# Three taps of a 31-tap depthwise convolution go from TensorE to VectorE

## The chip, the cores and the metric

The kernel runs on one core of one Trainium2 chip, in one launch, with float32 inputs and outputs. The metric is the device time of one execution in microseconds (us). Of the engines, PE is TensorE, DVE is VectorE, ACT is ScalarE, POOL is GpSimd, and SP issues the transfers.

## The reference

The reference is a first block (modulation, a two-branch mixer, a gated feed-forward part), and then two more layers (gated delta rule, block attention, each with a SwiGLU part). The change lies in one branch of the first mixer, on 256 positions of 512 channels:

```python
h = layer_norm(x) * (1.0 + sc1[:, None]) + sh1[:, None]
proj = h @ w_in[l]
a_val, a_gate, u_pool, gate_a, gate_b = jnp.split(proj, [...], axis=-1)
ya = a_val * jax.nn.sigmoid(a_gate)
ya = causal_dwconv(ya, w_dw_a[l], b_dw_a[l])      # 31 taps, 512 channels, one filter per channel
ya = jax.nn.silu(layer_norm(ya, ln_a_g[l], ln_a_b[l]))
ya = ya @ w_pw_a[l]
...                                               # a pooling branch makes yb
merged = jax.nn.sigmoid(gate_a) * ya + jax.nn.sigmoid(gate_b) * yb
mix = merged @ w_out[l]
```

Everything after `mix` depends on it: the other layers work on this block's output.

## The kernel before

Activations lie with channels on the 128 partitions and the 256 positions along the row, in tiles of 128 x 256. Weights stream in as units of 128 x 1024 float32 in the order of a fixed plan, into a ring of eleven buffers `raw`. For each unit ACT makes a rounded copy `hi` (`high`, line 1119) and DVE the remainder `lo = raw - hi` (`low`, line 1652), each into a ring of five slots. A product is then three matmuls, hi by hi, hi by lo and lo by hi (`three`, line 542). One output tile of 128 x 256 takes 8 x 3 = 24 matmuls. DVE runs `low` four units ahead of the unit that PE is at, and `high` for a unit waits until PE has finished the unit five before it. Some buffers of the ring hold rows of the modulation matrix, which DVE alone consumes (`ada`, line 1639).

No scheduler orders the work: each engine's queue is written out by hand, and the engines meet at semaphores. In the stage around the change the loop over `n` from 0 to 7 makes the input-projection tiles 20 to 27 (they are called so here), whose outputs are the gates of the pooling branch. Beside each tile some taps of the convolution are done.

A tap on PE is four float32 matmuls (line 644), one per channel tile: the stationary operand is a 128 x 128 diagonal matrix with the tap's weights, which ACT makes from the identity (line 1195), the moving operand the shifted input `ypad` (in the profile Z). They all add up in two PSUM banks. The trace records a float32 matmul as two instructions. `TAPS_AT[n]` says how many taps stand behind which tile; its entries 7 to 12 belong to the tiles 22 to 27. A tap on DVE is four operations `cv = ypad * w + cv` on 128 x 256 (line 1767; `cv` is B in the profile), each waiting for the one of the tap before on the same channel tile. Both engines work at the same convolution without waiting for each other; at the stage's end DVE adds the two PSUM banks to `cv` (line 1824), for which it waits for the last tap of both. Then comes a layer norm over channels (PE line 549 for the mean), in which PE is kept running with matmuls whose results nobody reads (`spin`, line 537), then SiLU, and the next product (`pw`).

In the loop DVE's queue for tile 20+n holds: `low`, for n = 7 also an `ada`, then tap or taps, then the multiplication of one pooled output by its gate (line 1818), which waits for ACT's sigmoid (line 1230) of an earlier tile. ACT's holds: `high`, the diagonals of the taps behind this tile, the sigmoid of the tile.

Of the kernel before, what the change touches and what calls it, by code (L numbers as in the profile page):

```python
# [262 lines left out]
class Marks:  # L263
# [12 lines left out]
    def up(self, name, key=0):  # L276
        chain = SEM_OF.get(name, name)
        n = self.count[chain] = self.count.get(chain, 0) + 1
        if self.counting:
            assert (name, key) not in self.place, (name, key)  # L280
            self.place[name, key] = n
        assert self.place[name, key] == n, (name, key)
        return self.sem(name), 1

    def at(self, name, key=0):
        return self.sem(name), 1 if self.counting else self.place[name, key]
# [33 lines left out]
def program(nc, wts, head, vecs, csts, rows, xtok, xT, low_dram, inv_dram, out):  # L320
    with ExitStack() as ctx:
# [37 lines left out]
        def V(name, i=0, n=1):  # L359
            return vec[:, VOFF[name] + i:VOFF[name] + i + n]  # L360
# [7 lines left out]
        up, at = marks.up, marks.at  # L368
# [17 lines left out]
        def acc(b0, n):  # L386
            return bank[(b0 + n // 2) % 8][:, (n % 2) * S:(n % 2) * S + S]
# [7 lines left out]
        def pair(b):  # L395
            return bank[b][:, :].rearrange("p (a b) -> p a b", a=2)
# [64 lines left out]
        xt = B[4][:, :, :].rearrange("p a b -> p (a b)").rearrange("p (c n) -> p c n", c=2)  # L461
        xh = B[5]
        xst, xmv, xrs, xnm = sm[:, 0:24].rearrange("p (c n) -> p c n", c=2), sm[:, 24:28], sm[:, 28:30], sm[:, 30:31]
        PE_TAPS = list(range(12, 31))
        TAPS_AT = {n: t for n, t in zip(range(1, 13), (1, 1, 1, 2, 2, 1, 2, 2, 2, 2, 2, 1))}


        def sync(g, s):
# [64 lines left out]
        def tensor(g, s):  # L533
# [105 lines left out]
            def conv(i):  # L639

                for t in range(4):
                    s.wait_ge(*at("diag", (i, t)))
                    s.wait_ge(*at("ya", t))
                    g.matmul(acc(0, t), cv[:, 4 + (n_diag[0] % 8) // 2, (n_diag[0] % 2) * P:(n_diag[0] % 2) * P + P],  # L644
                             ypad[:, t, 2 + i:2 + i + S], start=i == PE_TAPS[0] and t % 2 == 0, stop=i == 30,
                             skip_group_check=True).then_inc(*up("conv", (i, t)))
                    n_diag[0] += 1
# [3 lines left out]
            def convs(n):  # L651
                for _ in range(TAPS_AT[n]):
                    conv(PE_TAPS[tap_n[0]])
                    tap_n[0] += 1
# [457 lines left out]
        def scalar(g, s):  # L1112
# [72 lines left out]
            def diagonals(n):  # L1185
                for _ in range(TAPS_AT[n]):
                    i = PE_TAPS[tap_n[0]]
                    tap_n[0] += 1
                    for t in range(4):
                        if n_diag[0] >= 8:  # L1190
                            s.wait_ge(*at("conv", diag_of[n_diag[0] - 8]))
                        d = cv[:, 4 + (n_diag[0] % 8) // 2, (n_diag[0] % 2) * P:(n_diag[0] % 2) * P + P]
                        diag_of.append((i, t))
                        n_diag[0] += 1
                        g.activation(d, ident, ACT.Copy, scale=V("w_dw_a", t * 31 + i)).then_inc(*up("diag", (i, t)))
# [434 lines left out]
        def vector(g, s):  # L1630
# [17 lines left out]
            def low(j):  # L1648

                if j < len(UNITS):  # L1650
                    s.wait_ge(*at("hi", j))
                    g.tensor_tensor(lo[:, j % SPLIT, :], raw[:, PLACE[j] % RAW, :], hi[:, j % SPLIT, :].bitcast(F),  # L1652
                                    ALU.subtract).then_inc(*up("lo", j))
                    for i in range(PLACE[j] + 1, PLACE[j + 1] if j + 1 < len(UNITS) else len(PLAN)):
                        if j > 15 and j != LATE:
                            ada(i)
# [102 lines left out]
            def tap(i):  # L1759
                for t in range(4):  # L1760
                    w, src = V("w_dw_a", t * 31 + i), ypad[:, t, 2 + i:2 + i + S]
                    if i == 0:
                        s.wait_ge(*at("ya", t))
                        g.tensor_scalar(cv[:, t, :], src, w, V("b_dw_a", t), ALU.mult, ALU.add).then_inc(*up("tap", (i, t)))
                    else:
                        s.wait_ge(*at("tap", (i - 1, t)))
                        g.scalar_tensor_tensor(out=cv[:, t, :], in0=src, scalar=w, in1=cv[:, t, :], op0=ALU.mult,  # L1767
                                               op1=ALU.add).then_inc(*up("tap", (i, t)))
# [12 lines left out]
            def pool_group(q):  # L1781
                if q < 4:
                    w = win[q % 2][:, q, 16:272]
                    s.wait_ge(*at("win", 3))
                    s.wait_ge(*cst_in)
                    g.tensor_tensor(h[:, q, 0:16], w[:, 0:16], C("icnt", q * 16, q * 16 + 16),
                                    ALU.mult).then_inc(*up("pool_edge", q))
                    g.scalar_tensor_tensor(out=h[:, q, 16:S], in0=w[:, 16:S], scalar=0.5 ** (q + 1),
                                           in1=up_pad[:, q, 32:272], op0=ALU.mult,
                                           op1=ALU.subtract).then_inc(*up("pool_rest", q))  # L1790
                    s.wait_ge(*at("pool_edge", q))
                    g.tensor_tensor(h[:, q, 0:16], h[:, q, 0:16], up_pad[:, q, 16:32],
                                    ALU.subtract).then_inc(*up("mean_pool", q))
                if q:
                    s.wait_ge(*at("pooled_hi", q - 1))
                    g.tensor_tensor(fl[:, q - 1, :], h[:, q - 1, :], fh[:, q - 1, :].bitcast(F),
                                    ALU.subtract).then_inc(*up("pooled", q - 1))
# [5 lines left out]
            for n in range(8):  # L1803
                if n == 2:
                    low(UNIT["pool", 0] + AHEAD)
                    pool_group(4)
                    tap(6)
                low(UNIT["in", 20 + n] + AHEAD)
                if n < 2:
                    pool_group(2 * n)  # L1810
                    pool_group(2 * n + 1)
                if n < 7:
                    tap(4 + n if n < 2 else 5 + n)
                if n > 1:
                    for i in (n - 2, n - 1) if n == 7 else (n - 2,):
                        s.wait_ge(*at("gate_b", i))
                        s.wait_ge(*at("yb", i))
                        g.tensor_tensor(yb[:, i, :], yb[:, i, :], ev[:, i % 4, :], ALU.mult).then_inc(*up("ybg", i))
            s.wait_ge(*at("gate_b", 7))
            g.tensor_tensor(yb[:, 7, :], yb[:, 7, :], ev[:, 3, :], ALU.mult).then_inc(*up("ybg", 7))  # L1820
            for b in range(2):
                s.wait_ge(*at("conv", (30, 3)))
                s.wait_ge(*at("tap", (11, 3)))
                g.tensor_tensor(cv[:, 2 * b:2 * b + 2, :], cv[:, 2 * b:2 * b + 2, :], pair(b),
                                ALU.add).then_inc(*up("conv_sum", b))

# [491 lines left out]
        for engine in (sync, gpsimd, scalar, tensor, vector):  # L2318
            engine(Counting(), Counting())
# [19 lines left out]
        @block.vector  # L2339
        def _(g):  # L2340
            vector(g, Waits(g))
# [105 lines left out]
```

## Time and profile before

| what | value |
|---|---|
| median of 3 runs | 1156.27 us (1154.5 to 1156.55) |
| the profiled execution's own time | 1159.28 us |
| its span, first to last instruction | 1157.5 us |
| PE busy | 1096.5 us, 95% |
| DVE busy | 792.8 us, 68% |
| ACT busy | 613.5 us, 53% |
| share of 16 DMA engines' time in use by the weights' queue | 49.7% |
| mean granted TensorE clock | 0.979 |

Busy shares are means over stages with different limits. What a change in one stage is worth is read in that stage: which engine has no idle time there, and for whom the operation at its end waits. The stage of the change runs from about 101 to 139 us. In a row of a timeline, the bracket at the end is the idle time of the engine ahead of the row, and the work that ended it; a float32 matmul counts twice in the number behind the x.

### The profile page before, as it was taken

To read this page: it belongs to the slowest core of one execution; us is meant where nothing else is said; L and a number is where in the kernel's file an instruction comes from. 1 tells how busy PE (TensorE), PEld (TensorE's weight loads), DVE (VectorE), ACT (ScalarE), POOL (GpSimd) and SP (SyncE) were. 2 spreads that over 40 slices of the span, in tenths; PEclk is the share of its full clock that TensorE was granted. 3 is DMA by queue.
4 is the path that set the end of the run, shared out by engine and by line. 5 is a ranking of instruction groups with operands and counts; after the bars stand their busy time and mean duration, and the time that the engine had idled before them with its cause. 6 is when DMAs were issued, how large, how long until landed. Compare 5 with 4: busy or idle time off the path is not lost.

```text
span 1157.5 us, 19080 instructions
## 1 busy us (share of the span) xinstructions
PE 1096.5 (95%) x7816; PEld 1027.4 (89%) x7816; DVE 792.8 (68%) x1349; ACT 613.5 (53%) x1039; POOL 3.3 (0%) x13
## 2 busy tenths in 40 slices
PE   7998988999999998879989999999999899999997
PEld 7998878899999988779988799999989787999996
DVE  7987488878887777586674745555588847555555
ACT  6567435465565548843344644444565537445453
POOL 0000000000000000000000000000000000000000
PEclk8999999999999998989999999999999999999999
DMA  9985246347666624144122455565555434555520
GB/s 378 418 322 165 91 146 255 103 155 244 241 214 210 203 71 133 35 125 147 65 86 70 132 199 192 184 190 184 177 183 164 127 109 166 197 186 183 195 75 37
DMA packets 58550, 195.49 MB, mean 169 GB/s; under 512 B 10848, under 2 KB 11232, under 8 KB 58208
## 3 DMA queue, kind: packets, MB, share of 16 engines
q1 hardware_dynamic: 58464, 194.28, 49.7%
q8 instruction: 62, 1.02, 0.3%
q14 instruction: 24, 0.20, 0.0%
HBM read 192.94 MB, written 1.31 MB: 168 GB/s over the span
## 4 chain that ended last, share of the span: by engine, by line
PE 74%; DVE 16%; ACT 7%; issue 2%; SPq 1%; DMA 0%; POOL 0%; ACTq 0%; DVEq 0%; POOLq 0%
PE ps L542 61%; DVE lo L1652 5%; PE ps L816 3%; ACT hi L1119 2%; PE ps L644 2%; DVE raw L1639 2%; PE ps L699 1%; PE ps L549 1%; DVE ev L1883 1%; PE ps L537 1%; DVE ev L1880 1%; DVE B L1661 1%; PE ps L822 1%; DVE B L1767 1%; SPq L510 1%
## 5 line engine op out<-in xcount | busy, mean ns | idle before, releaser
L1652 DVE TENSOR_TENSOR lo<-raw,hi 128x1024 fp32r<-128x1024 f32 x311 | 377.4, 1222 | 168.4 <-ACT hi L1119 167.5
L542 PE MATMUL ps<-hh,hi 128*128 128x256 f32 x1568 | 448.3, 286 | 14.4 <-DVE hl L1744 3.2
L542 PE MATMUL ps<-hh,lo 128*128 128x256 f32 x1568 | 441.9, 282 | 0.0
L542 PE MATMUL ps<-hl,hi 128*128 128x256 f32 x1568 | 441.4, 282 | 0.0
L1119 ACT ACTIVATE hi<-raw 128x1024 fp32r<-128x1024 f32 x311 | 323.5, 1052 | 58.3 <-PE ps L542 58.2
L542 PEld LDWEIGHTS ps<-hh,hi 128*128 128x128 f32 x1568 | 298.9, 191 | 19.9 <-issue 9.6
L542 PEld LDWEIGHTS ps<-hl,hi 128*128 128x128 f32 x1568 | 298.8, 191 | 1.9
L542 PEld LDWEIGHTS ps<-hh,lo 128*128 128x128 f32 x1568 | 298.7, 190 | 0.0
L1350 ACT ACTIVATE ev<-ps 128x256 f32<-128x256 f32 x72 | 27.7, 385 | 109.8 <-PE ps L542 109.8
L542 PE MATMUL ps<-hi,fh 128*128 128x512 f32 x192 | 76.3, 397 | 0.0
L542 PE MATMUL ps<-lo,fh 128*128 128x512 f32 x192 | 75.9, 395 | 0.0
L542 PE MATMUL ps<-hi,fl 128*128 128x512 f32 x192 | 75.8, 395 | 0.0
L542 PE MATMUL ps<-hi,hh 128*128 128x512 f32 x176 | 72.4, 411 | 2.9 <-DVE hl L1926 2.5
L542 PE MATMUL ps<-lo,hh 128*128 128x512 f32 x176 | 69.8, 397 | 0.0
L542 PE MATMUL ps<-hi,hl 128*128 128x512 f32 x176 | 69.7, 396 | 0.0
L1639 DVE CUSTOM_DVE_ANT_0 raw<-raw,crow 128x1024 f32<-128x1024 f32 x48 | 58.3, 1220 | 0.1
L542 PE MATMUL ps<-fh,hi 128*128 128x256 f32 x184 | 52.6, 286 | 2.5 <-ACT B L1223 2.5
L542 PE MATMUL ps<-fh,lo 128*128 128x256 f32 x184 | 51.8, 282 | 0.0
L542 PE MATMUL ps<-fl,hi 128*128 128x256 f32 x184 | 51.7, 281 | 0.0
L2039 DVE SCALAR_TENSOR_TENSOR B<-ps,vec,B 128x255 f32<-128x255 f32 (+2 forms) x72 | 34.6, 481 | 20.5 <-ACT B L1435 18.8
L542 PEld LDWEIGHTS ps<-hi,hh 128*128 128x128 f32 x176 | 33.4, 190 | 11.9 <-issue 3.8
L542 PEld LDWEIGHTS ps<-lo,fh 128*128 128x128 f32 x192 | 36.1, 188 | 8.5
(277 smaller groups left out, 1349.7 us busy)
## 6 DMA issues: line engine op xcount, KB each, us to landing
raw<-in_w SPq DMA_DIRECT2D x359, 512.0 KB, 4.3
B<-in_t SPq DMA_DIRECT2D x2, 512.0 KB, 4.2
xa<-in_x SPq DMA_DIRECT2D x1, 1024.0 KB, 11.3
B<-in_r SPq DMA_DIRECT2D x1, 1024.0 KB, 6.1
out<-h SPq DMA_DIRECT2D x4, 256.0 KB, 2.0
cst<-in_c SPq DMA_DIRECT2D x1, 864.0 KB, 9.3
B<-between SPq DMA_DIRECT2D x32, 4.0 KB, 1.7
vec<-in_v SPq DMA_DIRECT2D x1, 328.5 KB, 7.1
```

The source lines that it names most:

```text
L510: g.dma_start(tm[d, 2 * c + q, :, d], inv_dram[q, 4 * c:4 * c + 4, b].rearrange("n i j -> i n j")).then_inc(s_tm[q], 16)
L537: g.matmul(bank[7][:, 0:S], idle[:, 0:P], idle[:, :], start=True, stop=True, skip_group_check=True)
L542: m = g.matmul(o, l, r, start=first and n == 0, stop=last and n == 2, skip_group_check=True)
L549: m = g.matmul(bank[bm][:, 0:S], ones[:, one, :], y[:, k, :], start=k == 0, stop=k == nch - 1, skip_group_check=True)
L644: g.matmul(acc(0, t), cv[:, 4 + (n_diag[0] % 8) // 2, (n_diag[0] % 2) * P:(n_diag[0] % 2) * P + P], ypad[:, t, 2 + i:2 + i + S], start=i = ...
L699: g.matmul(bank[2 * c + k // 4][:, (k % 4) * P:(k % 4) * P + P], xa[:, k, c * P:c * P + P], C("alpha"), start=k % 4 == 0, stop=False, skip ...
L816: m = g.matmul(bank[b][:, i * P:i * P + P], left(i), right(i), start=i == 0, stop=True, skip_group_check=True)
L1119: g.activation(hi[:, j % SPLIT, :], raw[:, PLACE[j] % RAW, :], ACT.Copy).then_inc(*up("hi", j))
L1350: g.activation(ev[:, t % 4, :], bank[4 + t % 4][:, 0:S], ACT.Copy if half else ACT.Silu).then_inc(*up("ff_out", (kup, t)))
L1639: g.tensor_tensor_reduce(r, r, crow[:, :], 1.0, 0.0, ALU.mult, ALU.add, mod[:, col:col + 1]).then_inc(*up("ada", n))
L1652: g.tensor_tensor(lo[:, j % SPLIT, :], raw[:, PLACE[j] % RAW, :], hi[:, j % SPLIT, :].bitcast(F), ALU.subtract).then_inc(*up("lo", j))
L2039: m = g.scalar_tensor_tensor(out=dst[:, d:], in0=bank[b][:, 0:S - d], scalar=V("a_conv", t * 4 + i), in1=dst[:, d:], op0=ALU.mult, op1=ALU ...
```

## The change

PE keeps 16 taps (15 to 30) and DVE gets 15 (0 to 14); before it was 19 and 12. The three taps are taken from behind the tiles 24, 25 and 26, where PE now does one tap instead of two. DVE's taps beside these three tiles become two each: 9 and 10, 11 and 12, 13 and 14. ACT makes twelve diagonals fewer. The final addition waits for DVE's tap 14 in place of 11. Nothing else in the program differs.

```diff
-        PE_TAPS = list(range(12, 31))
-        TAPS_AT = {n: t for n, t in zip(range(1, 13), (1, 1, 1, 2, 2, 1, 2, 2, 2, 2, 2, 1))}
+        PE_TAPS = list(range(15, 31))
+        TAPS_AT = {n: t for n, t in zip(range(1, 13), (1, 1, 1, 2, 2, 1, 2, 2, 1, 1, 1, 1))}
...
                 if n < 7:
-                    tap(4 + n if n < 2 else 5 + n)
+                    for i in (4 + n,) if n < 2 else (5 + n,) if n < 4 else (2 * n + 1, 2 * n + 2):
+                        tap(i)
...
-                s.wait_ge(*at("tap", (11, 3)))
+                s.wait_ge(*at("tap", (14, 3)))
```

In DVE's queue before, beside the tiles 24 to 27 and up to the final addition (line 1652 is `low`, 1767 a tap, 1818 and 1820 gate multiplications, 1639 an `ada`):

```order
L1652 TENSOR_TENSOR lo<-raw,hi 128x1024
L1767 SCALAR_TENSOR_TENSOR B<-Z,vec,B 128x256 x4
L1818 TENSOR_TENSOR B<-B,ev 128x256
L1652 TENSOR_TENSOR lo<-raw,hi 128x1024
L1767 SCALAR_TENSOR_TENSOR B<-Z,vec,B 128x256 x4
L1818 TENSOR_TENSOR B<-B,ev 128x256
L1652 TENSOR_TENSOR lo<-raw,hi 128x1024
L1639 ISA raw,mod<-raw,crow 128x1024
L1639 ISA mod 128x1
L1818 TENSOR_TENSOR B<-B,ev 128x256 x2
L1820 TENSOR_TENSOR B<-B,ev 128x256
L1824 TENSOR_TENSOR B<-B,ps 128x512 x2
```

These rows begin with the queue's part of tile 25. The same part now (every line number past the edit is one higher):

```order
L1652 TENSOR_TENSOR lo<-raw,hi 128x1024
L1767 SCALAR_TENSOR_TENSOR B<-Z,vec,B 128x256 x8
L1819 TENSOR_TENSOR B<-B,ev 128x256
L1652 TENSOR_TENSOR lo<-raw,hi 128x1024
L1767 SCALAR_TENSOR_TENSOR B<-Z,vec,B 128x256 x8
L1819 TENSOR_TENSOR B<-B,ev 128x256
L1652 TENSOR_TENSOR lo<-raw,hi 128x1024
L1639 ISA raw,mod<-raw,crow 128x1024
L1639 ISA mod 128x1
L1819 TENSOR_TENSOR B<-B,ev 128x256 x2
L1821 TENSOR_TENSOR B<-B,ev 128x256
L1825 TENSOR_TENSOR B<-B,ps 128x512 x2
```

Each run of four tap operations became one of eight, ahead of the gate multiplication and of the next `low`; the part of tile 24 changed in the same way.

In PE's queue, the end of tile 24 with its taps and the start of tile 25, before (ps0 and ps1 are the banks of the convolution, ps2 that of tile 24):

```order
L542 MATMUL ps2<-hh,lo 128x256
L644 MATMUL ps0<-Z,B0 128x256 x2
L644 MATMUL ps1<-Z,B0 128x256 x2
L644 MATMUL ps0<-Z,B0 128x256 x2
L644 MATMUL ps1<-Z,B0 128x256 x2
L542 MATMUL ps3<-hh,hi 128x256
```

and now:

```order
L542 MATMUL ps2<-hh,lo 128x256
L644 MATMUL ps0<-Z,B0 128x256 x2
L644 MATMUL ps1<-Z,B0 128x256 x2
L542 MATMUL ps3<-hh,hi 128x256
```

Four diagonal matmuls went from between two tiles; the same happened behind the tiles 25 and 26.

## Rows read from the trace of the kernel before

**Rows 1.** The profile's page, busy engines and the chain that ended last.
```profile
PE 1096.5 (95%) x7816; PEld 1027.4 (89%) x7816; DVE 792.8 (68%) x1349; ACT 613.5 (53%) x1039; POOL 3.3 (0%) x13
PE 74%; DVE 16%; ACT 7%; issue 2%; SPq 1%; DMA 0%; POOL 0%; ACTq 0%; DVEq 0%; POOLq 0%
```

**Rows 2.** The chain in order of time: start, us, what.
```profile
118.36 3.46 PE ps L644 x16
121.81 2.81 PE ps L542 x24
...
137.15 1.74 PE ps L644 x8
```

**Rows 3.** Timeline of PE, taps behind tile 24 and the start of tile 25.
```profile
118.19 3.62 PE L644 MATMUL ps<-Z,B 128*128 128x256 f32 x16
121.46 0.47 PE L542 MATMUL ps<-hh,hi 128*128 128x256 f32 x1
```

**Rows 4.** Timeline of DVE from tile 24 to the final addition.
```profile
113.50 1.23 DVE L1652 TENSOR_TENSOR lo<-raw,hi 128x1024 fp32r<-128x1024 f32 x1 [3.15 <-ACT hi L1119]
114.64 1.67 DVE L1767 SCALAR_TENSOR_TENSOR B<-Z,vec,B 128x256 f32<-128x256 f32 x4
116.22 0.42 DVE L1818 TENSOR_TENSOR B<-B,ev 128x256 f32<-128x256 f32 x1
119.75 1.23 DVE L1652 TENSOR_TENSOR lo<-raw,hi 128x1024 fp32r<-128x1024 f32 x1 [3.11 <-ACT hi L1119]
120.90 1.67 DVE L1767 SCALAR_TENSOR_TENSOR B<-Z,vec,B 128x256 f32<-128x256 f32 x4
...
132.28 1.23 DVE L1652 TENSOR_TENSOR lo<-raw,hi 128x1024 fp32r<-128x1024 f32 x1 [3.11 <-ACT hi L1119]
133.42 1.22 DVE L1639 CUSTOM_DVE_ANT_0 raw<-raw,crow 128x1024 f32<-128x1024 f32 x1
134.56 0.08 DVE L1639 DVE_READ_ACCUMULATOR2_ANT mod<- 128x1 f32 x1
134.56 0.76 DVE L1818 TENSOR_TENSOR B<-B,ev 128x256 f32<-128x256 f32 x2
137.60 0.42 DVE L1820 TENSOR_TENSOR B<-B,ev 128x256 f32<-128x256 f32 x1 [2.28 <-ACT ev L1230]
138.91 1.29 DVE L1824 TENSOR_TENSOR B<-B,ps 128x512 f32<-128x512 f32 x2 [0.89 <-PE ps L644]
```

**Rows 5.** Timeline of ACT, beside tile 25 and at the stage's end.
```profile
118.67 1.05 ACT L1119 ACTIVATE hi<-raw 128x1024 fp32r<-128x1024 f32 x1
119.62 2.63 ACT L1195 ACTIVATE B<-first,vec 128x128 f32<-128x128 f32 x8
...
137.18 0.38 ACT L1230 ACTIVATE ev<-ps 128x256 f32<-128x256 f32 x1 [3.77 <-PE ps L542]
```

**Rows 6.** Line 1767 (taps on DVE): duration ns, least/median/most.
```profile
L1767 DVE SCALAR_TENSOR_TENSOR B<-Z,vec,B x44: 476/481/490, 74.5 to 128.3; 128x256 f32<-128x256 f32 x44
```

**Rows 7.** All waits of the core, longest first: the rows that name a transfer.
```profile
PEld ps L822 <- DMA B<-between: 6.0, 1, 6.0
PE ps L822 <- DMA B<-between: 5.8, 1, 5.8
DVE sm L1717 <- DMA B<-in_t: 5.0, 1, 5.0
```

**Rows 8.** Timeline of PE at the two products that follow an idle time.
```profile
97.03 0.38 PE L542 MATMUL ps<-fh,hi 128*128 128x256 f32 x1 [2.47 <-ACT B L1223]
...
153.05 0.36 PE L542 MATMUL ps<-hh,hi 128*128 128x256 f32 x1 [2.82 <-DVE hl L1836]
```

**Rows 9.** Stretches: PE, PEld, DVE, ACT, POOL busy, granted clock, DMA share, GB/s.
```profile
97.00:101.00 4.00, 3.97 (x17) 3.62 (x18) 3.11 (x8) 2.34 (x6) 0.00 (x0) 0.57 0.69 205
140.00:153.00 13.00, 9.98 (x68) 9.36 (x68) 6.17 (x11) 5.49 (x11) 0.00 (x0) 1.00 0.01 1
153.00:165.00 12.00, 11.54 (x96) 11.37 (x96) 10.85 (x17) 4.17 (x5) 0.00 (x0) 1.00 0.62 191
600.00:616.00 16.00, 10.92 (x61) 10.85 (x60) 10.74 (x25) 8.76 (x14) 0.00 (x0) 0.69 0.19 55
912.00:928.00 16.00, 12.72 (x68) 11.06 (x67) 9.87 (x31) 8.01 (x20) 0.00 (x0) 0.89 0.31 99
```

## The prediction

> **What bounds the kernel now.** I began with the page: PE is busy 95% of the span and carries 74% of the chain that ended last; transfers carry 0% of it [rows 1]. That is an average, so the second view is the chain in order of time around the change. There it is PE without a break: from tile 24 on, tap matmuls (line 644, 16 records, 3.46 us) alternate with the 24 matmuls of a tile (line 542, 2.81 us), up to the last 8 records, after which DVE's addition at line 1824 starts [rows 2, 4]. The reader is to see that no DVE or ACT piece stands between them. The third view, PE's timeline, shows the same stage without a bracket of idle time: the taps behind tile 24 start at 118.19 and tile 25 at 121.46 [rows 3]. The fourth is DVE's timeline. Beside each of these tiles DVE does a `low`, four tap operations and a gate multiplication and then idles 3.11 to 3.15 us, until ACT has made the next `hi`, which itself waits for PE to finish a tile. At the end DVE waits 0.89 us for PE's last tap before the addition [rows 4]. So PE is the bound of this stage and DVE has spare time in the very places the taps are moved to.
>
> **What is removed from PE.** Three taps of four matmuls, 12 float32 matmuls or 24 records. The chain gives 3.46 us for 16 records, 0.216 us each, so one tap (8 records) is 1.73 us; its last row, 8 records in 1.74 us, says the same directly [rows 2]. Three taps are 3 x 1.73 = 5.19 us. They leave from between tiles that stand back to back, so PE's end of the stage moves forward by all of it, if nobody makes PE wait instead. With them go 12 diagonals on ACT: eight took 2.63 us beside tile 25 [rows 5], so about 1.2 us less per tile. ACT was not on the chain here; I count that as nothing.
>
> **What is added to DVE, and whether it fits.** A tap of four operations starts at 114.64 and the next instruction at 116.22: 1.58 us, or 0.395 us per operation [rows 4]. Twelve more make 4.74 us. PE's period per tile falls from 6.27 (2.81 + 3.46) to 2.81 + 1.73 = 4.54 us. DVE's work per tile becomes 1.14 (`low`, 113.50 to 114.64) + 8 x 0.395 = 3.16 + about 0.37 (gate multiplication) = 4.67 us. That is 0.13 us more than PE's period, so the idle time of DVE vanishes and it lags a little. Whether the lag matters has to be followed with times:
> - Tile 24: `low` at 113.50, taps to 117.80, done at 118.17. Unchanged before it, since PE moves only from 119.92 on.
> - Tile 25: its `low` needs the `hi` that follows the end of tile 24's 24 matmuls; that is not moved, so it starts at 119.75 as before [rows 4]. Done at 119.75 + 4.67 = 124.42.
> - Tile 26: PE has finished tile 25's matmuls 1.73 us earlier, so `hi` would allow 126.02 - 1.73 = 124.29 (126.02 is one period of 6.27 behind 119.75); DVE is free at 124.42 and starts then. Done at 129.09.
> - Tile 27: `hi` would allow 132.28 - 3.46 = 128.82; DVE starts at 129.09. `low` and `ada` take 2.28 us (132.28 to 134.56), the two gate multiplications 0.72: done at 132.09.
> - The last gate multiplication waits for ACT's sigmoid of tile 27, which PE now releases 5.19 earlier: 137.60 - 5.19 = 132.41. It takes 0.42, to 132.83.
> - PE's last tap allows the addition at 138.91 - 5.19 = 133.72.
>
> So DVE's own last work is ready 0.89 us before PE, as it was, and the addition starts at 133.72. The lag of DVE by 0.27 us is still 0.32 short of where it would delay even the last gate multiplication. Does the lag reach PE another way? `low` runs four units ahead, so a `lo` late by 0.27 us is not waited for by any tile; tile 27's bank comes free with the sigmoid of tile 23. ACT's sigmoid of tile 27 needs the gate multiplication of 3, done at 124.42 and wanted at about 132. Nothing queued behind the longer run of taps is needed sooner.
>
> **Bounds of a tap operation in a run of eight.** The trace shows runs of four only. The lower bound is the pitch of 0.395 us. The upper is a full duration each, median 0.481 us [rows 6], if the operations stopped overlapping. Then DVE's work per tile is 1.14 + 3.85 + 0.37 = 5.36: tile 25's part ends at 125.11, tile 26's at 130.47, tile 27's at 133.47, the last gate multiplication at 133.89 and the addition starts there instead of at 133.72, a loss of 0.17 us. I take the pitch, since a run of eight is the same operation in the same pattern, each depending on the fourth before it: the gain is 5.19 with it and 5.02 without.
>
> The Trainium skill, in "VectorE: DVE Perf Modes", section "The TRN2 errata — SBUF-src ops pay a fixed extra latency per instruction", speaks against the change: many small operations each pay a fixed latency that lies between instructions, so narrow pieces are a poor way to use DVE. The trace shows an overlap (pitch 0.395 against a duration of 0.481), which the rule as told does not give; by the rule the sum would be 5.02, by the row 5.19.
>
> **Behind the stage.** Everything later depends on the addition through the layer norm. ACT's table load stands behind the sigmoid of tile 27 and moves with it. Transfers: from 140 to 153 us the DMA share is 0.01, everything wanted had landed long before, and the only waits for a transfer in the whole trace are one at the start and one small round trip in the delta rule [rows 7, 9]. So the rest moves forward as it stands. Sum for the profiled execution: 1159.28 - 5.19 = 1154.09 us. That execution is 3.01 us above the median of the runs; by the median, 1156.27 - 5.19 = 1151.1 us.
>
> **Rivals.**
> - *PE meets a slower clock behind the norm.* After an idle time of 2.47 us at 97.03 the granted clock was 0.57 for 4 us, part of the time at 1.2 GHz instead of 2.4; after a longer one of 2.82 at 153.05 it stayed at 1.00 [rows 8, 9]. So the length of the idle time alone doesn't decide, and a stage that begins 5.19 us sooner may draw otherwise. Price by the first: 4 x 0.43 = 1.7 us. By the pair of like norms in the two late layers (0.69 and 0.89 over 16 us): 3.2 us [rows 9]. Against it: the idle times themselves are not changed, and before's own runs, which draw too, lie within 2.1 us. The time is then 1151.1 + 1.7 to 3.2 = 1152.8 to 1154.3, and as well 1149.4 to 1147.9 when it goes the other way. The Trainium skill ("TensorE: Matmul & The Clock Gate", section "Part 1: The HAM clock gate (the \"warmup\" mystery)") says that the chip watches activity on a window of its own, not started by the kernel; these rows agree in so far as the longer idle time was the harmless one.
> - *DVE becomes the bound.* For it: its work per tile exceeds PE's period by 0.13 us. At 0.481 each it costs 0.17 us (above), 1151.3. Only beyond that does it show: at 0.55 each, for which no row speaks, a tile's part is 1.14 + 4.40 + 0.37 = 5.91 us, and the addition starts at 119.75 + 2 x 5.91 + 2.28 + 0.72 + 0.42 = 134.99, a loss of 1.27: 1152.4.
> - *The gain is taken back by a later wait*, on the weight stream say: no change, 1155 to 1156.3. For it: a DMA share of 0.62 right after the stage [rows 9]. Against: no wait for `raw` in the trace [rows 7].
> - *Slower.* One mechanism: the clock behind the norms and in the delta rule, where PE idles most, is granted at the lower level more often. It needs 5.19 + 2.3 us, three times the 1.7 to 3.2 of a single place, more than before's runs ever spread. From 1158.6 on.
>
> **How the numbers follow.** What a measurement of this kernel can tell from no change is 0.2%, 2.3 us. Full gain with the clock as it was 0.67, a clock draw of either sign 0.15, DVE as the bound 0.06, taken back 0.07, slower 0.05. The predicted time is that of the first, 1151.1. The range reaches down to the smaller favourable draw less half a microsecond, 1148.9, and up to 1153.9, which holds the DVE rival and most of the unfavourable draws. Faster by over 0.2% (under 1153.96): the first, the DVE rival and most draws, 0.86; within 0.2%: the one taken back and the rest of the draws, 0.09; slower 0.05.
>
> **What would show it.** PE without idle time from tile 24 to the last tap, the tiles 25, 26 and 27 starting about 4.54 us apart, and the addition near 133.7 with PE named as what it waited for. DVE: eight tap operations in about 3.2 us, idle times of 3.1 us gone or below 0.2 beside tiles 26 and 27. Line 644 with 128 records, line 1767 with 56. Wrong if DVE is the releaser of the addition's stretch (its last gate multiplication ending after PE's last tap), if the run of eight takes over 3.85 us, if PE waits for `lo` at a tile, or if the stage ends 5 us sooner and the kernel does not.

## The result, and the profile after

The changed kernel took 1152.83 us, the median of 7 runs (1151.13 to 1154.76), against 1156.27 us for the kernel before, 7 runs (1154.5 to 1157.38). The ratio is 0.9965 with a 95% interval of 0.9951 to 0.9979: faster, by 2.4 to 5.7 us. I had predicted 1151.1, in a range of 1148.9 to 1153.9.

The profiled execution took 1152.83 us with a span of 1151.0. The chain of waits in order of time around the stage (start, us, what), which answers to [rows 2]:

```profile
113.58 2.80 PE ps L542 x24
116.38 1.73 PE ps L644 x8
118.11 2.80 PE ps L542 x24
120.91 1.73 PE ps L644 x8
122.64 2.80 PE ps L542 x24
125.43 1.73 PE ps L644 x8
127.16 2.81 PE ps L542 x24
129.97 1.74 PE ps L644 x8
131.73 1.30 DVE B L1825 x2
```

The chain is still PE's alone. Behind the tiles 24, 25 and 26 stand 8 records of line 644 where 16 stood, 1.73 us in place of 3.46, and the tiles follow each other at 4.53 us.

DVE's timeline from tile 24's `low` to the final addition, which answers to [rows 4]:

```profile
111.52 1.23 DVE L1652 TENSOR_TENSOR lo<-raw,hi 128x1024 fp32r<-128x1024 f32 x1 [3.12 <-ACT hi L1119]
112.66 3.25 DVE L1767 SCALAR_TENSOR_TENSOR B<-Z,vec,B 128x256 f32<-128x256 f32 x8
115.83 0.42 DVE L1819 TENSOR_TENSOR B<-B,ev 128x256 f32<-128x256 f32 x1
117.78 1.23 DVE L1652 TENSOR_TENSOR lo<-raw,hi 128x1024 fp32r<-128x1024 f32 x1 [1.53 <-ACT hi L1119]
118.92 3.25 DVE L1767 SCALAR_TENSOR_TENSOR B<-Z,vec,B 128x256 f32<-128x256 f32 x8
122.09 0.41 DVE L1819 TENSOR_TENSOR B<-B,ev 128x256 f32<-128x256 f32 x1
122.42 1.22 DVE L1652 TENSOR_TENSOR lo<-raw,hi 128x1024 fp32r<-128x1024 f32 x1
123.56 3.25 DVE L1767 SCALAR_TENSOR_TENSOR B<-Z,vec,B 128x256 f32<-128x256 f32 x8
126.73 0.41 DVE L1819 TENSOR_TENSOR B<-B,ev 128x256 f32<-128x256 f32 x1
127.07 1.22 DVE L1652 TENSOR_TENSOR lo<-raw,hi 128x1024 fp32r<-128x1024 f32 x1
...
130.42 0.42 DVE L1821 TENSOR_TENSOR B<-B,ev 128x256 f32<-128x256 f32 x1 [0.32 <-ACT ev L1230]
131.73 1.28 DVE L1825 TENSOR_TENSOR B<-B,ps 128x512 f32<-128x512 f32 x2 [0.89 <-PE ps L644]
```

Read the brackets. Beside tiles 26 and 27 (122.42 and 127.07) there is none: DVE works without a pause. A run of eight goes from 112.66 to 115.83, 3.17 us. The last gate multiplication still waits 0.32 us for ACT, and the addition 0.89 us for PE, as before: DVE is full, but PE still ends the stage. Line 644 has 128 records in this trace and line 1767 has 56, as forecast.

From tile 24's `low`, which nothing of the change precedes, to the addition it is 131.73 - 111.52 = 20.21 us; before it was 138.91 - 113.50 = 25.41 [rows 4]. That is 5.20 us. The whole difference of the two spans is 1157.5 - 1151.0 = 6.5 us, and splits at four points of the two timelines:

| stretch | before | after | difference |
|---|---|---|---|
| start to tile 24's `low` | 113.50 | 111.52 | -1.98 |
| to the final addition | 25.41 | 20.21 | -5.20 |
| to the first matmul of `pw` | 14.14 | 14.14 | 0.00 |
| from there to the end | 1004.45 | 1005.13 | +0.68 |

The first line can't come from the change, for all of it lies ahead of the change. About half of it, 1.05 us, is there before the pooling product starts (at 97.03 before [rows 8], here at 95.98): between 20 and 40 us the granted clock was 0.94 before and 1.00 here. The other 0.93 us lie between that start and tile 24's `low` (16.47 us and 15.54): the pooling product ran at 0.57 before [rows 9], here at 1.00. The last line holds differences of this kind both ways, the first of them at the start of `pw`. The stretches of four microseconds at the start of `pw`, of the kernel before, of the changed one, and of a second execution of the changed one (busy PE, PEld, DVE, ACT, POOL, granted clock, DMA share, GB/s):

```profile
153.05:157.05 4.00, 4.00 (x34) 4.00 (x35) 3.90 (x8) 1.78 (x2) 0.00 (x0) 1.00 0.01 4
```
```profile
145.87:149.87 4.00, 4.00 (x21) 4.00 (x22) 3.90 (x8) 0.94 (x1) 0.00 (x0) 0.57 0.08 8
```
```profile
147.94:151.94 4.00, 4.00 (x34) 4.00 (x35) 3.90 (x8) 1.80 (x2) 0.00 (x0) 1.00 0.08 9
```

34 matmuls begin in four microseconds at the full clock, 21 in the same time when most of it is at 1.2 GHz. The first 72 matmuls of `pw`, in the chains of the two kernels:

```profile
153.05 8.73 PE ps L542 x72
```
```profile
145.87 10.27 PE ps L542 x72
```

The lower clock cost the changed kernel 1.54 us here, in this execution. The third row shows that it is not bound to the change.

Some 14 to 16 us after the start of `pw` the next product starts, behind 2.81 us of idle time of PE in both kernels, and behind that product a later layer norm (line 549). The first eight microseconds of that product and the first four of that norm, in the kernel before:

```profile
167.40:175.40 8.00, 8.00 (x68) 8.00 (x69) 6.86 (x19) 3.76 (x11) 0.00 (x0) 1.00 0.29 117
193.15:197.15 4.00, 4.00 (x11) 3.30 (x12) 3.83 (x9) 0.00 (x0) 0.00 (x0) 0.59 1.03 418
```

and in the changed one:

```profile
161.76:169.76 8.00, 8.00 (x55) 8.00 (x56) 6.84 (x19) 3.76 (x11) 0.00 (x0) 0.79 0.24 94
187.49:191.49 4.00, 4.00 (x20) 3.54 (x21) 4.00 (x10) 0.00 (x0) 0.00 (x0) 1.00 1.03 422
```

In the changed kernel that product was slower at first (0.79) and left PE 1.54 us of idle time ahead of the norm; in the kernel before it was not (1.00) and left 2.80 us. This cost or gained nothing, because the norm waits for DVE: it starts 25.73 and 25.75 us after the product's start. But behind the longer idle time the norm met the lower clock, and from its start to the next product it took 29.37 us before and 27.76 here. All fourteen traces of this case, those of the experiments included, fall into two such groups. Four (the kernel before; after_third, five_taps and before_spin2 below) had 1.00 in the product, 2.70 to 2.81 us of idle time and 0.57 to 0.59 in the norm; ten had 0.62 to 0.82, 0.37 to 1.80 us, and 1.00. PE's old stage and the shortened one are in both groups. So the last line of the table is 1.54 us more at `pw`, 1.6 us less at this norm, and 0.8 us more in all the rest.

So the traces say 5.2 us for the change; the medians said 3.44 for the time being. The experiments had to find out whether the rest is a draw of the clock or a loss.

### The profile page after: what moved, and what is told of

It reads as the page before. It is cut to its first block, busy times and chain, and to the rows that moved or that the text cites. A ratio compares the mean times of both kernels' runs of the same rounds, so it can differ in the third digit from the quotient of the medians.

```text
span 1151.0 us, 19032 instructions
## 1 busy us (share of the span) xinstructions
PE 1090.4 (95%) x7792; PEld 1022.6 (89%) x7792; DVE 796.9 (69%) x1361; ACT 608.5 (53%) x1027; POOL 3.3 (0%) x13
## 4 chain that ended last, share of the span: by engine, by line
PE 73%; DVE 16%; ACT 7%; issue 2%; SPq 1%; DMA 0%; POOL 0%; ACTq 0%; DVEq 0%; POOLq 0%
PE ps L542 61%; DVE lo L1652 5%; PE ps L816 3%; ACT hi L1119 2%; DVE raw L1639 2%; PE ps L699 1%; PE ps L644 1%; DVE ev L1884 1%; PE ps L537 1%; DVE ev L1881 1%; PE ps L549 1%; DVE B L1661 1%; PE ps L822 1%; DVE B L1767 1%; SPq L510 1%
```

## The experiments

Two measures are given for each: the ratio of times to the kernel before with its 95% interval, and from its trace the stretch from tile 24's `low` to the addition ("the stage": 25.41 us before, 20.21 after).

**1. The changed kernel again, two sets.** No edit.

> The changed kernel once more, nothing altered. The stage is 5.20 us shorter in its trace, yet the median fell by 3.44 us (interval 2.4 to 5.7). Theory 1, the whole 5.19 us is passed on and the first product behind the norm met the lower clock by a draw: the trace shows either clock behind the norm from one execution to another, and the difference of the medians lies anywhere from 3.5 to 5.2 us. Theory 2, the moved stage meets the lower clock in every execution because its times are 5 to 7 us earlier: clock about 0.6 for some 3.5 us behind the norm again, difference about 3.5 us. Theory 3, some 1.7 us are taken back by a wait later on: the clock behind the norm may be 1.00 and still the difference is about 3.5 us.

Ratio 0.9962 (0.9947 to 0.9977). The stage took 133.80 - 113.55 = 20.25 us. The clock behind the norm was 1.00 (third row above), which was theory 1's sign and excludes theory 2, that it is lost every time. From `pw`'s first matmul to the end it took 1003.46 us; the half on DVE alone (experiment 2), which has PE's old stage and the same clock at `pw` and at the two places behind it, took 1003.66. So nothing was taken back behind the norm in this trace.

> The changed kernel once more beside it. The trace says 5.2 us in the stage; two sets of runs said 3.44 (interval 2.4 to 5.7) and 4.4 (2.7 to 6.1). Theory 1, the whole is passed on: a third interval that holds 5.2 us, ratio near 0.9955. Theory 3, 1.7 us are taken back: near 0.9970.

Ratio 0.9954 (0.9938 to 0.9969), stage 133.96 - 113.72 = 20.24 us, clock behind the norm 0.61. All three intervals hold 0.9955, the 5.2 us of the traces. The one near 0.9970 that theory 3 called for did not come, though only the third interval excludes it, and barely. The mean of the three ratios is 0.9960, 4.6 us.

**2. Each half of the change alone.** First PE and ACT only:

```diff
-        PE_TAPS = list(range(12, 31))
+        PE_TAPS = list(range(15, 31))
-        TAPS_AT = {... (1, 1, 1, 2, 2, 1, 2, 2, 2, 2, 2, 1))}
+        TAPS_AT = {... (1, 1, 1, 2, 2, 1, 2, 2, 1, 1, 1, 1))}
```

> The change on PE and ACT alone: 16 taps on PE (15 to 30), DVE keeps its 12; the taps 12 to 14 are left out of the sum. My theory, that DVE's added taps cost nothing: the part from tile 24's low to the final addition is 20.2 us, as in the changed kernel, against 25.4 before, and the median that of the changed kernel. Rival, that DVE's part costs some 1 to 2 us somewhere (in the stage or behind it): shorter than the changed kernel by that.

Ratio 0.9963 (0.9947 to 0.9979), stage 131.91 - 111.70 = 20.21 us: to the hundredth that of the changed kernel. DVE's idle time beside tiles 26 and 27 is what was left for the taps:

```profile
117.96 1.23 DVE L1652 TENSOR_TENSOR lo<-raw,hi 128x1024 fp32r<-128x1024 f32 x1 [3.11 <-ACT hi L1119]
...
122.49 1.23 DVE L1652 TENSOR_TENSOR lo<-raw,hi 128x1024 fp32r<-128x1024 f32 x1 [1.38 <-ACT hi L1119]
...
127.01 1.23 DVE L1652 TENSOR_TENSOR lo<-raw,hi 128x1024 fp32r<-128x1024 f32 x1 [1.38 <-ACT hi L1119]
```

Each gap of 1.38 us is less than a tap's 1.58. The rest is the lag, and it is covered by the wait at the end.

Then DVE only: the `tap` loop and the wait of the changed kernel, the two tables of the kernel before.

> The change on DVE alone: PE keeps 19 taps, DVE gets its 15, so the taps 12 to 14 are added twice. My theory: 25.4 us from tile 24's low to the final addition, as before, DVE's idle time beside tiles 25, 26 and 27 about 1.5 us each in place of 3.1, ratio to before 1.000. Rival: slower than before, by up to 1 to 2 us.

Ratio 0.9995 (0.9982 to 1.0007), stage 135.30 - 109.89 = 25.41 us, as before to the hundredth, idle times of 1.52 and 1.53 us. Twelve more operations on DVE cost nothing. The two halves add up: all of the gain is PE's 5.2 us.

**3. The same taps in another place.** PE as in the changed kernel; DVE does the extra ones beside tiles 19, 20 and 21.

```diff
             for n in range(4):
                 low(UNIT["in", 16 + n] + AHEAD)
                 window(n)
                 tap(n)
+                if n == 3:
+                    tap(4)
...
-                    for i in (4 + n,) if n < 2 else (5 + n,) if n < 4 else (2 * n + 1, 2 * n + 2):
+                    for i in (2 * n + 5, 2 * n + 6) if n < 2 else (8 + n,):
```

The tap beside the pooling product is number 9 in this one.

> The changed kernel's division of taps, but DVE does its three extra ones early: beside tiles 19, 20 and 21, with the rest of its taps moved up accordingly, and one each beside the tiles 22 to 26. The chain of before ran over DVE up to 97 us, with the taps on it. My theory, DVE's time is free only where it idles: the part up to tile 24's low becomes longer by two to three taps of 1.58 us, 3.2 to 4.7 us, the part behind it is 20.2 us as in the changed kernel, and of the gain of 5.2 only 0.5 to 2.0 us are left. Rival, the place does not matter: as the changed kernel.

Ratio 0.9997 (0.998 to 1.0015): 0.3 us faster by the ratio, with an interval from 2.3 us faster to 1.7 us slower. That is less than the changed kernel's 4.6 us, but it cannot tell the 0.5 to 2.0 us that I expected from none at all. The part behind tile 24's `low` took 139.04 - 118.80 = 20.24 us, as it should. The part ahead of it took 118.80, 5.0 to 8.9 us more than in the traces of the other kernels (109.89 to 113.79), where I had 3.2 to 4.7. PE's timeline at the pooling product, and the clock of the eight microseconds there, show why it can be more:

```profile
100.32 0.39 PE L542 MATMUL ps<-fh,hi 128*128 128x256 f32 x1 [4.04 <-ACT B L1223]
```
```profile
100.00:104.00 4.00, 3.16 (x14) 2.61 (x15) 4.00 (x8) 2.48 (x6) 0.00 (x0) 0.63 0.25 85
104.00:108.00 4.00, 4.00 (x15) 3.39 (x14) 2.33 (x5) 3.27 (x9) 0.00 (x0) 0.51 0.55 183
```

PE stood still for 4.04 us, 2.47 before [rows 8], which is one tap of DVE more. At 91.85 us it had already stood still for 2.07 us, against 0.49 at the same place before: one tap again. And then it worked longer at the lower clock: the kernel before had 0.89 from 100 to 104 us and 1.00 from 104 to 108. DVE's time is free only where DVE idles, and where it does not, PE is made to wait and pays twice.

**4. Past the limit.** Three taps on DVE beside each of tiles 24 to 26, none on PE behind them.

```diff
-        PE_TAPS = list(range(15, 31))
+        PE_TAPS = list(range(18, 31))
-        TAPS_AT = {... (1, 1, 1, 2, 2, 1, 2, 2, 1, 1, 1, 1))}
+        TAPS_AT = {... (1, 1, 1, 2, 2, 1, 2, 2, 0, 0, 0, 1))}
...
-                    for i in (4 + n,) if n < 2 else (5 + n,) if n < 4 else (2 * n + 1, 2 * n + 2):
+                    for i in (4 + n,) if n < 2 else (5 + n,) if n < 4 else (3 * n - 3, 3 * n - 2, 3 * n - 1):
...
-                s.wait_ge(*at("tap", (14, 3)))
+                s.wait_ge(*at("tap", (17, 3)))
```

> The same move carried past the limit: PE does no tap behind the tiles 24 to 26 (13 in all), DVE three beside each (18 in all). DVE's work per tile is 1.14 + 12 x 0.395 + 0.37 = 6.25 us against PE's 2.81, so DVE is the bound: from tile 24's low 3 x 6.25 + 2.28 + 0.72 + 0.37 = 22.1 us to the final addition, which then follows the last gate multiplication; 1.9 us longer than the changed kernel, 3.3 shorter than before. If the time of a tap operation grew in long runs (0.481 us), it would be 25.2 us, no gain left.

The stage took 133.46 - 111.45 = 22.01 us, against 22.1 expected: a run of twelve operations keeps the pitch of 0.395 us. DVE, and PE at the norm:

```profile
117.72 1.23 DVE L1652 TENSOR_TENSOR lo<-raw,hi 128x1024 fp32r<-128x1024 f32 x1
118.86 4.83 DVE L1767 SCALAR_TENSOR_TENSOR B<-Z,vec,B 128x256 f32<-128x256 f32 x12
...
133.12 0.42 DVE L1821 TENSOR_TENSOR B<-B,ev 128x256 f32<-128x256 f32 x1
133.46 1.28 DVE L1825 TENSOR_TENSOR B<-B,ps 128x512 f32<-128x512 f32 x2
```
```profile
134.79 3.78 PE L549 MATMUL ps<-B,ones 128*128 128x256 f32 x8 [8.35 <-DVE B L1825]
```

The addition has no bracket: nobody but DVE itself is in front of it. Yet the ratio was 0.9991 (0.9976 to 1.0006), 1 us instead of the 3.4 that the stage gained. In the trace the greater part of the loss is plain: PE had idled 8.35 us, was granted 0.50 over the next four microseconds and took 3.78 us for the norm's first 8 records, 1.99 in the changed kernel's trace. From the addition to `pw` it was 16.11 us in place of 14.14, so 1.97 of the 3.4 us went there. My expectation counted the stage alone.

**5. The idle time behind the norm filled.** 22 more unread matmuls in this norm, in the changed kernel and in the kernel before, two sets each.

```diff
                 if warm:
-                    spin(38)
+                    spin(60 if nid == "ya" else 38)
```

> The changed kernel with 60 unread matmuls in place of 38 in the norm of this stage, 22 x 0.118 = 2.6 us, which fill PE's idle time of 2.82 us ahead of the next product. By theories 1 and 2 the product behind it runs at clock 1.00, and the median is up to 1.7 us under that of the changed kernel (all of it by theory 2, part by theory 1): about 1151.1 to 1152. By theory 3 nothing changes, 1152.8.

> The kernel before with the same 60 unread matmuls. Its trace showed clock 1.00 behind this norm. Theory 2: no gain, ratio 1.000. Theory 1: it too draws the lower clock in some executions, so a gain of a fraction of 1.7 us. Against after_spin the difference should be the whole 5.2 us by both; by theory 3 it is 3.5.

> The changed kernel with 60 unread matmuls in the norm, a second set beside the kernel before with the same. Open is whether the filled idle time brings more to the moved stage (2.4 us by the medians so far, 0.9939 against about 0.9960) than to the stage where it was (0.3 us, 0.9997). If the moved stage meets the lower clock more often: again 2 us or more under the changed kernel, ratio 0.994 or less. If the clock behind the norm is an even draw for both, this kernel and the other gain alike, about half of 1.7 us: ratio near 0.9950 here.

> The kernel before with 60 unread matmuls in the norm, beside the above on the same chip. Even draw: ratio near 0.9993. If the stage in its old place never meets the lower clock: 1.000. Against the other kernel of this call the difference is the stage's 5.2 us if nothing else differs.

PE's idle time ahead of `pw` fell from 2.82 to 0.19 us, here in the first of the changed kernel's:

```profile
144.57 0.35 PE L542 MATMUL ps<-hh,hi 128*128 128x256 f32 x1 [0.19 <-DVE hl L1837]
```
```profile
144.57:148.57 4.00, 4.00 (x34) 4.00 (x35) 3.90 (x8) 1.79 (x2) 0.00 (x0) 1.00 0.06 5
```

The clock behind the norm was 1.00 in all five traces with the filled idle time (the four sets here and the one of experiment 6). In the nine without, all with 2.82 or 2.83 us of idle time, it was 1.00 in three and 0.50 to 0.61 in six. So in these traces the filling kept the clock, and without it the clock differed between executions of one and the same kernel, the changed one (0.57, 1.00 and 0.61), and was more often low than high. The times follow less clearly. The changed kernel with it: 0.9939 (0.9918 to 0.9961) and 0.9951 (0.9934 to 0.9968), mean 0.9945 against 0.9960 without, 1.7 us better, which is no more than the intervals of the two means leave open. The kernel before with it: 0.9997 (0.9982 to 1.0013) and 1.0004 (0.999 to 1.0018), no gain. With the filled time on both sides, the stage's move is 0.9945, 6.4 us (7.6 and 7.1 by the medians of the two pairs); without, 0.9960, 4.6 us; the traces' 5.2 lies between (the stage took 25.41 us in both filled traces of the kernel before and 20.24 in both of the changed one), and the intervals of the four sets, some 2 us to either side of 6.4, hold it.

No one of the theories has all four of its numbers. The first median of the changed kernel, 1150.27, lies below the 1151.1 to 1152 that I had expected. The second ratio, 0.9951, is that of the even draw. The kernel before, with no gain twice, is as if it never met the lower clock. What is shown is the clock in the traces; that it is what moved the medians is not.

Of the nine traces, the two with PE's old stage showed 1.00, and of the seven with the shortened one, six the lower clock. That suggests that the shortened stage meets it more often. Two against seven do not show it.

**6. Two taps more, and all together.** PE keeps 14 taps. DVE's two further ones stand beside the pooling product, where it idled 2.66 us before, and beside tile 23.

```diff
-        PE_TAPS = list(range(15, 31))
+        PE_TAPS = list(range(17, 31))
-        TAPS_AT = {... (1, 1, 1, 2, 2, 1, 2, 2, 1, 1, 1, 1))}
+        TAPS_AT = {... (1, 1, 1, 2, 2, 1, 1, 1, 1, 1, 1, 1))}
...
                     pool_group(4)
                     tap(6)
+                    tap(7)
...
-                    for i in (4 + n,) if n < 2 else (5 + n,) if n < 4 else (2 * n + 1, 2 * n + 2):
+                    for i in (4 + n,) if n < 2 else (8,) if n == 2 else (2 * n + 3, 2 * n + 4):
...
-                s.wait_ge(*at("tap", (14, 3)))
+                s.wait_ge(*at("tap", (16, 3)))
```

> The changed kernel with two more taps moved from PE to DVE, 14 and 17: PE does one tap instead of two behind the tiles 22 and 23 too; DVE does its extra ones beside the pooling product, where it had 1.8 to 2.7 us of idle time, and beside tile 23, where it had 3.1. By my theory (a tap is 1.73 us of PE, and 1.58 us of DVE that cost nothing while DVE has idle time there): DVE's work per tile of 4.67 us against PE's 4.54 lets it lag by 0.1 per tile, the last gate multiplication still waits for the sigmoid or nearly, and the stage is 3.46 us shorter than in the changed kernel, the median 3.0 to 3.5 us lower, about 1149.4 (1147.6 with the whole 8.65 us against before). The rival, that DVE is at its limit already: the addition starts after DVE's last multiplication and the gain over the changed kernel is under 1.5 us.

Ratio 0.9943 (0.9925 to 0.996), 1150.25 us. From tile 22's `low` to the addition it was 130.53 - 103.04 = 27.49 us against 138.91 - 102.77 = 36.14 before: 8.65 us, the expected number. In the changed kernel's trace with the same clock at the pooling product (after_third) the same part took 133.96 - 102.99 = 30.97 us, 3.48 more, where 3.46 was expected. Against the changed kernel of the same set, 1153.80 us, the median is 3.55 us lower, by the ratios 2.2; 3.0 to 3.5 was expected. DVE has no idle time left from 103.04 on but 0.15 us ahead of the last gate multiplication (128.32 + 0.75 = 129.07) and the wait for PE:

```profile
128.32 0.75 DVE L1820 TENSOR_TENSOR B<-B,ev 128x256 f32<-128x256 f32 x2
129.22 0.42 DVE L1822 TENSOR_TENSOR B<-B,ev 128x256 f32<-128x256 f32 x1
130.53 1.28 DVE L1826 TENSOR_TENSOR B<-B,ps 128x512 f32<-128x512 f32 x2 [0.89 <-PE ps L644]
```

> Five taps moved and the 22 further unread matmuls in the norm together, the version that the runs so far point to. Both the stage (8.65 us shorter in the trace of the five taps) and the clock behind the norm (1.00, up to 1.7 us where it was drawn low) should count: 8.65 plus 0 to 1.7 us under before, 1147.4 to 1149.2 against 1157.8, ratio 0.991 to 0.9925. If what the unread matmuls seem to bring is only spread between runs, the ratio is that of the five taps, 0.9943, again.

Ratio 0.9915 (0.9896 to 0.9935), median 1148.61 us against 1157.48 for the kernel before on the same chip: 8.9 us (9.8 by the ratio), within the expected 8.65 to 10.35. The part from tile 22's `low` is again 27.49 us (130.27 - 102.78) and the clock behind the norm 1.00. It beats both kernels, the changed one beside it (1153.26) by 4.65 us. How much of the 0.0028 between it and the five taps without the filling is due to the filling stays open: the two intervals overlap.

## Why the prediction was right

**What bounds the stage, and the sum.** PE did, and does. The removed taps were worth 5.20 us in the trace (5.19 in the sum), and the half on PE alone gives the same stage to the hundredth.

**DVE's cover.** Followed with times, it came out as written. From tile 24's `low` on I had put tile 25's 6.25 us later, tile 26's 10.92, tile 27's 15.59 and the last gate multiplication 18.91; they were 6.26, 10.90, 15.55 and 18.90. The last wait for ACT was forecast at 0.32 us and was 0.32, the wait for PE at 0.89 and was 0.89. The run of eight kept the pitch, 3.17 us where 3.16 was taken, so the upper bound of 0.481 each did not come true; nor did it in a run of twelve. By the rule of the Trainium skill ("VectorE: DVE Perf Modes", section "The TRN2 errata — SBUF-src ops pay a fixed extra latency per instruction") the prediction had put the gain at 5.02. The trace does not follow it here: 5.20, with operations that start every 0.396 us (3.17 / 8).

**Behind the stage.** Here the sum was thin: "everything moves forward as it stands" held for the layer norm (14.14 us in both), but not for the clock. It also held for transfers, though [rows 7] were not all the waits for one, as the prediction says: the same view has a fourth, of DVE at line 2074, 2.3 us before and 1.4 after. The first rival happened in the profiled execution: lower clock behind the norm, 1.54 us, where I had put 1.7 as its price. I had given a draw of either sign 15%, on the strength of a single trace of before with 1.00. In nine traces with that idle time six had the lower clock, and all six were among the seven with the shortened stage. What the prediction called the likeliest case, full gain "with the clock as it was", is therefore not what most of these traces show, and the difference of the median from it, 1152.83 to 1151.1, is 1.7 us. That the clock behind this norm explains all of it is not shown: the kernel before lost 1.6 us at the later norm, where the changed one lost nothing; the three ratios of the same kernel (0.9965, 0.9962, 0.9954) differ by 1.3 us among themselves, and before's own runs spread over 9 us (1152.62 to 1161.86 in one set of 27). The range was wide enough for the whole gain and for the gain less such a loss, so that the time alone could not have told them apart. That the mechanism was right is known from the stage, not from the median.

**The other rivals.** DVE as the bound: not with two taps beside a tile, but with three. Taken back later: no; with like clocks, the part behind the norm took 1003.46 us with the shortened stage and 1003.66 with the old one. Slower: no.

## What to carry to other kernels

Work goes to the engine that idles only where it idles, and the place is read from the brackets of that engine's timeline, not from its busy share: the same three taps gave 5.2 us of stage beside tiles that left DVE 3.1 us each, and no gain of time clear of the noise where DVE was on the chain. The receiving engine may even exceed the bound's period a little, as long as the lag at the end of the stage is smaller than the wait that stands there. Compare stretches between fixed points of two traces before believing a difference of medians of 0.3%, and look at more than one trace before calling the clock behind an idle time the usual one. A lower clock costs time only where PE is the one waited for: at the product behind `pw` it cost nothing, at the norm behind that 1.6 us.

## What had not been expected of the hardware

- The granted clock after one and the same idle time of PE (2.82 or 2.83 us) was 1.00 in three traces and 0.50 to 0.61 in six. With the idle time cut to 0.18 or 0.19 us it was 1.00 in five of five.
- Likewise behind the wait of 2.46 or 2.47 us at the pooling product, ahead of the change, up to which thirteen of the fourteen traces have the same program: 1.00 in seven of them, 0.74 in one and 0.57 in five, the kernel before among these [rows 9].
- A slower stretch can spare a later one: where the product behind `pw` had 1.00, PE then idled 2.70 to 2.81 us and the norm behind it met 0.57 to 0.59 (four of four); where it had 0.62 to 0.82, PE idled 0.37 to 1.80 us and the norm had 1.00 (ten of ten).
- DVE and PE read the same `ypad` at the same time in longer runs with no effect on either: 0.395 us per tap operation and 0.216 us per record, as before.
